# Two transformer blocks on one core: stage boundaries cut into units of two k-tiles, last steps by token block, context normed ahead of its stage

## The reference

```python
# first block
h = rmsnorm(x, pre_mix_g);  p = h @ w_in                        # 4368 columns
o = concat(rmsnorm(window_attention(p)), rmsnorm(forgetting_attention(p)))
x = x + rmsnorm(o @ w_out, post_mix_g)
h = rmsnorm(x, pre_ffn_g);  u = conv3(h @ w_up)                 # 2 * 5632 columns
x = x + rmsnorm((gelu(gate(u)) * val(u)) @ w_down, post_ffn_g)
# second block: six modulation vectors of 2048 from c, and from c_ctx
sh_a, sc_a, g_a, sh_m, sc_m, g_m = split(silu(c) @ w_ada + b_ada)
h  = rms_norm(x, norm_attn_w) * (1 + sc_a) + sh_a
hc = rms_norm(ctx, norm_attn_w) * (1 + csc_a) + csh_a           # 256 context rows
q, k, v, u = split(h @ w_in_2)                                  # 2560 columns; k, v of hc too
x = x + g_a * (concat(attention(q, k, v, kc, vc), pool(u) @ pool_w * pool_scale) @ w_out_2)
x = x + g_m * (relu(modulate(rms_norm(x, norm_mlp_w)) @ w_mlp_up) ** 2 @ w_mlp_down)
return rms_norm(x, final_norm_w)
```

## Time and profile before

| what | value |
|---|---|
| median of 3 runs | 2277.32 us (2276.34 to 2283.1) |
| the profiled execution | 2285.57 us, of it the span 2283.9 us |
| mean granted TensorE clock | 0.974 |
| TensorE busy | 2182.5 us, 96% of the span |
| VectorE, ScalarE, GpSimd busy | 1521.3, 1064.6, 135.2 us |
| mean DMA | 211 GB/s |

### The profile page before, as it was taken

How to read it: one execution, slowest core, us unless ns; L and a number is a source line. 1 busy time by engine, 2 the same in 40 slices (tenths; PEclk the granted TensorE clock), 3 DMA queues, 4 the chain that set the end, 5 groups by cost and what they waited for, 6 DMA issues and landing times.

```text
span 2283.9 us, 30297 instructions
## 1 busy us (share of the span) xinstructions
PE 2182.5 (96%) x10232; PEld 1807.2 (79%) x10232; DVE 1521.3 (67%) x1845; ACT 1064.6 (47%) x1379; POOL 135.2 (6%) x233
## 2 busy tenths in 40 slices
PE   7999998999999999999978999889999999999997
PEld 6888776788778888888867778777888888888876
DVE  6987788687895887768665364556655555655655
ACT  5444654555433554345456355345434434444442
POOL 2101000101010101100000000001000000000000
PEclk9998999999998999999999999899999999999999
DMA  8985077788786888977645250465756756766652
GB/s 283 305 292 188 1 233 263 231 267 267 254 281 207 276 273 276 310 247 240 205 147 184 86 184 1 147 203 192 232 185 211 240 193 211 233 199 205 222 182 94
DMA packets 267022, 482.51 MB, mean 211 GB/s; under 512 B 14861, under 2 KB 107349, under 8 KB 265633
## 3 DMA queue, kind: packets, MB, share of 16 engines
q1 hardware_dynamic: 236544, 367.18, 48.1%
q0 software_dynamic: 30192, 113.72, 15.8%
...
HBM read 478.81 MB, written 2.11 MB: 211 GB/s over the span
## 4 chain that ended last, share of the span: by engine, by line
PE 93%; ACT 3%; DVE 2%; issue 1%; DMA 0%; DVEq 0%; ACTq 0%
PE G L1416 28%; PE G L1418 28%; PE G L1417 28%; PE T L1463 1%; PE T L1600 1%; PE T L1709 1%; PE T L1452 1%; PE T L1541 1%; ACT junk L498 1%; PE G L1689 1%; ACT w_hi L548 1%; PE G L1534 1%; PE T L1564 0%; DVE h_lo L941 0%; PE G L1730 0%
## 5 line engine op out<-in xcount | busy, mean ns | idle before, releaser
L868 DVE TENSOR_TENSOR w_lo<-raw,w_hi 128x1024 fp32r<-128x1024 f32 x696 | 844.0, 1223 | 481.3 <-ACT w_hi L548 477.0
L548 ACT ACTIVATE w_hi<-raw 128x1024 fp32r<-128x1024 f32 x696 | 735.4, 1060 | 913.5 <-PE G L1418 911.1
L1416 PE MATMUL G<-w_hi,h_hi 128*128 128x512 f32 (+1 forms) x1920 | 754.6, 393 | 17.1 <-ACT w_hi L548 7.1
L1418 PE MATMUL G<-w_hi,h_lo 128*128 128x512 f32 (+1 forms) x1920 | 749.4, 390 | 0.0
L1417 PE MATMUL G<-w_lo,h_hi 128*128 128x512 f32 (+1 forms) x1920 | 749.3, 390 | 0.0
L1416 PEld LDWEIGHTS G<-w_hi,h_hi 128*128 128x128 f32 x1920 | 363.9, 190 | 95.1 <-issue 11.3
L1418 PEld LDWEIGHTS G<-w_hi,h_lo 128*128 128x128 f32 x1920 | 363.6, 189 | 75.3
L1417 PEld LDWEIGHTS G<-w_lo,h_hi 128*128 128x128 f32 x1920 | 363.8, 189 | 72.9
L1416 PE MATMUL G<-w_hi,a_hi 128*128 128x512 f32 x896 | 353.4, 394 | 5.6 <-ACT w_hi L548 4.2
L1418 PE MATMUL G<-w_hi,a_lo 128*128 128x512 f32 x896 | 350.8, 392 | 0.0
L1417 PE MATMUL G<-w_lo,a_hi 128*128 128x512 f32 x896 | 350.7, 391 | 0.0
(11 more groups left out here) (233 smaller groups left out, 1173.2 us busy)
## 6 DMA issues: line engine op xcount, KB each, us to landing
ada_w<-in_w_ada POOLq DMA_DIRECT2D x192, 512.0 KB, 5.0
raw<-in_w_up SPq DMA_DIRECT2D x176, 512.0 KB, 6.0
raw<-in_w_mlp_up SPq DMA_DIRECT2D x128, 512.0 KB, 4.7
raw<-in_w_mlp_down SPq DMA_DIRECT2D x128, 512.0 KB, 4.7
raw<-in_w_in SPq DMA_DIRECT2D x104, 512.0 KB, 5.2
raw<-in_w_down SPq DMA_DIRECT2D x88, 512.0 KB, 5.9
raw<-in_w_out SPq DMA_DIRECT2D x64, 512.0 KB, 4.8
raw<-in_w_in SPq DMA_DIRECT2D x8, 272.0 KB, 4.1
```

What stands on the lines that cost most here:

```text
L548: act.activation(w_hi[:, s % 4], raw[:, s // 2 % 4, STEPK * (s % 2):STEPK * (s % 2) + STEPK, :], ACT.Copy).then_inc(hi_ready, 1)
L868: dve.tensor_tensor(w_lo[:, s % 4], raw[:, s // 2 % 4, STEPK * (s % 2):STEPK * (s % 2) + STEPK, :], w_hi[:, s % 4].bitcast(F32), ALU.subtr ...
L1416: pe.matmul(out, ah, wh, start=f, stop=False)
L1418: mm = pe.matmul(out, al, wh, start=False, stop=l)
```

## The change

Units of two k-tiles take the place of groups of four at each boundary (`UNITS = 8`, each unit its own T bank). Where there is no shift, h_hi and h_lo are made straight from PSUM. `begin`, one on each of the three engines, writes transposes, the first three steps, and the weight parts of the next steps between the units. Raw weights lie in 8 slots of 2 k-tiles, and a load is four DMAs of 256 KB.

```diff
@@ load (SyncE)
-            if l >= 4:
-                sp.wait_ge(lo_ready, 2 * l - 6 + 2 * d)
-            for k in range(2):
...
+            for half in range(2):
+                s = 2 * l + half
+                if s >= 8:
+                    sp.wait_ge(lo_ready, s - 7 + 2 * d)
+                for k in range(2):
...
+                        dst, part = raw[:, s % 8, k, 0:src.shape[2]], src[:, STEPK * half + k, :]
+                    sp.dma_start(dst, part).then_inc(raw_full[s % 8], 16)
@@ TensorE
+        def begin(name, src, s, parity, ready):
+
+            turns(name, src, 0, 3)
+            steps(s, 0, 1, parity, H, ready)
+            turns(name, src, 3, 5)
+            steps(s, 1, 2, parity, H, ready)
+            turns(name, src, 5, 7)
+            steps(s, 2, 3, parity, H, ready)
+            turns(name, src, 7, 8)
```

```diff
+        def last_steps(s, acts, kt, ready):
...
+            for b in range(NB):
+                for k in range(2):
+                    for j in range(STEPK):
...
+                        pe.matmul(G[:, 2 + b, :], ah, wh, start=False, stop=False)
...
+                if b == 0:
+                    mm.then_inc(block_done, 1)
```

```diff
-            for k in range(8):
+            for k in range(3 if c == 0 else 0, 7 if c == 3 else 8):
                 lo(s0 + 8 * c + 3 + k)
-                if k % 2:
-                    ada_op(1, 4 * c + k // 2)
+                if (k in (5, 7) if c == 0 else k in (0, 1, 2, 3) if c == 3 else k % 2):
+                    ada_op(2, tile)
+                    tile += 1
```

```diff
+            def context():
+                if c >= 1:
+                    act.wait_ge(ctx_in, 16)
+                    for g in (2 * c - 2, 2 * c - 1):
+                        squares(g, lambda b: cx[:, b, g * N:g * N + N], sums=sqc)
+                if c == 2:
+                    root("ctx")
...
+            pool.tensor_scalar(cx[:, b, :], cx[:, b, :], rstdc[:, b:b + 1], None, ALU.mult).then_inc(ctx_scaled, 1)
...
+            residual(q, (lambda b: u_buf[:, b, (q - 6) * UCOLS:(q - 5) * UCOLS]) if q >= 6 else None)
+            dve.wait_ge(x_new, X_NEW["in2"] + q + 1)
+            in2_scale(q)
...
+        for q in range(UNITS):
+            turn("ctx", cx, q)
+            step(s0 + 8 + q, 1, H, STEPK * q, q == 0, q == 7, None)
```

```diff
+        for q, more in enumerate(((4,), (5, 6), (7,))):
+            steps(s0, q, q + 1, 0, H, r)
+            for m in more:
+                mix(m)
...
+        root("final", rstdx[:])
+        for b in range(NB):
+            for c in (0, 2):
+                dve.tensor_scalar(y[:, b, c * N:c * N + N], y[:, b, c * N:c * N + N], rstdx[:, b:b + 1], None,
```

980 lines of the change are left out of this document (611 added, 369 removed).

## The result

The changed kernel takes 2258.93 us, the median of four runs (2256.68 to 2260.77), beside 2279.47 for the kernel before, measured on the same chip (four runs, 2276.34 to 2283.1). The ratio is 0.9909, with a 95% interval of 0.9889 to 0.9929: it gained 20.5 us, some 16 to 25, where 39.2 were forecast. The time lies 2 us above the range's upper end of 2257.

A forecast was written before the change was run, and what follows sets the result against it. TensorE, busy for 96% of the span, was taken to bound the kernel. Gains less losses by boundary summed to 39.2 us, from the profiled 2285.6 to 2246, or 2238 on the median's scale; range 2224 to 2257.

The forecast's parts named there:

- the context: In the chunk with the context's transposes, transposes need only their units' banks: 8 us saved.
- out2: Attention 2 to out2: attention's half is split first and the mix fills time between steps, 11.5 us saved.
- the end: After the last stage: less work on the path and stores by block leave 11.2 us of 15.0, 3.8 saved.
- the term of -2 from down1c to in2: Boundary before in2: first step at t + 16 (t = previous step's end), but later steps wait; 2 us lost.
- rival C: At the boundaries, units gain less, through GpSimd contention or boundaries 3 us worse each; up to 2257 us, chance 0.18.
- the moved sum, "+1": First modulation sum moved from ahead of attention 1 to behind its scores: 1 us gained, between 0 and 4.
- out1's last two steps, "some 2.6 us": In out1's last chunk, four modulation tiles on VectorE make the last low part come some 2.6 us late.
- out2 to mlp2: Boundary before mlp2: block 0 evacuated early, table loaded ahead, first step at t + 7.2; 5.6 us saved.
- Attention to out1: Attention 1 to out1: first step at t + 4.1, 3.5 of waits, some 2 for the clock; 3.3 us saved.
- B: Before in2: the context does not hold down1c, so in2 begins 7 to 9 us sooner; 2230 us, chance 0.15.
- D: Weight loads: 256 KB DMAs take longer per byte, so TensorE waits; 2256 to 2305 us, chance 0.06.
- E: Last step pairs: VectorE is late, blocks save nothing; 5 us or less gained overall, 2273 us, chance 0.06.

The follow-up runs named there:

- after: The changed kernel itself, against the kernel before: 2258.93 us, ratio 0.9909.
- ctx_half: Changed kernel with GpSimd scaling only block 0 of the context, VectorE block 1 behind in2's units; 2252.11 us, ratio 0.9885 to the kernel before.
- ctx_late: Changed kernel with GpSimd's two context scalings moved behind in2's last unit; 2254.63 us, ratio 0.9896 to the kernel before.
- sum_back: Changed kernel with the first modulation sum put back ahead of attention 1; 2254.74 us, ratio 0.9894 to the kernel before.
- tiles_apart: Changed kernel with out1's last four modulation tiles behind low parts 0, 1, 5, 6, not 0 to 3; 2255.0 us, ratio 0.9871 to the kernel before.
- three: Changed kernel with VectorE scaling the context behind in2's opening, plus the changes of sum_back and tiles_apart; 2238.49 us, ratio 0.9822 to the kernel before.
- plain_last: Changed kernel with the last two steps of out1, down1c, out2, mlp2 not by block; 2259.3 us, ratio 0.9921 to the kernel before.
- loads_512: Changed kernel with raw weights loaded in DMAs of 512 KB, not 256 KB; 2256.7 us, ratio 0.9891 to the kernel before.

## Why the prediction was wrong

**The boundaries** were right, but for the one before in2 and the wait in out1: first steps at t + 4.2, 5.4 and 7.5 for 4.1, 5.7 and 7.2, the context +8.1 for 8, out2 +11.7 for 11.5, the end 10.8 for 11.2 us. Only the first step of in2 was not at t + 16 but at 24.4.

**The step that failed most: contention, in the term of -2 from down1c to in2.** Under rival C the prediction bounded it by nothing and by GpSimd's time of 4 to 8 us in full, and said "I keep the low end in the sum". It is 8.5 us to the first step and 9.9 to in2's third chunk, so even above the upper bound. No row stood behind the 4 to 8: GpSimd took 10.87 for its two scalings. The reason given was that "GpSimd waits only for the context's root and can be through before the second block's products". It waited for that root, but so does the high part that stands behind the root in ScalarE's program: GpSimd started at t + 0.2 and VectorE's low part at t + 0.8. The order of ScalarE's instructions, shown ahead of the prediction, put these two side by side, and the low end of "nothing" was not open. The rule cited there, the Trainium skill, GPSIMD Engine Reference, Specifications, said it: the trace agrees, with a low part of two inputs at 4.16 us for 1.23. The Trainium skill, SBUF — State Buffer, SBUF: two separate sides, is sharper: it has an exclusive lock that whichever comes first keeps for the whole instruction. The traces agree in the main: what was held began its work only 1.9 us before the end of a scaling of 5.44 (after, ctx_half), and in ctx_late GpSimd was the one held. Who came first cannot be read from GpSimd's rough spans.

One more thing in this term was read wrongly and did no harm. The high part behind the context's root was taken for that of down1c's last step. Both parts of that step were there in time, and no wait stands ahead of the last two steps, against what the last part of the prediction wanted to see; the high part is that of in2's second step. Block 0 was still taken only at t + 2.8 without GpSimd, as forecast (t + 3), since the same instruction stands ahead of its evacuation on VectorE: there a right number came out of a wrong reading.

**The second: the moved sum, "+1", between 0 and 4.** No gain, 6.8 us lost, on the wrong side of both ends. Two things were missed. The matmuls cost TensorE their time wherever they stand, 10.7 us inside and 12.0 ahead, against 6.2 by which attention began sooner. And the clock fell behind them: sum_back, which has the sum ahead, has 1.00 where after has 0.56. The clock is the larger part, by what one execution shows. In ctx_half the sum stands inside attention too, but the lower clock held only for some 4 us behind it: its halves took 3.73 and 3.84 us, and from in1's end to attention's end it is 76.2 us, 1.1 more than before and not 6.8. The prediction counted the lower clock only behind idle gaps. The trace of before could have told otherwise. The 10.83 us of the earlier trace rows are themselves a mean of both levels (the two halves at the upper one take 7.6 us), and amid up1b's products a sum of 64 such matmuls begins at 715.16 and takes 11.57 us; around its end and behind it TensorE was busy throughout, at 0.72:

```profile
720.00:740.00 20.00, 20.00 (x82) 17.50 (x83) 12.61 (x21) 3.83 (x5) 0.00 (x0) 0.72 0.34 107
```

**The third: out1's last two steps, "some 2.6 us".** 4.5 and 1.7 of clock. VectorE's sum of four tiles and low parts was right, but it took every tile's load as landed, though VectorE's idle time ahead of such tiles, 62.9 us for one kind of them, stands in the earlier trace rows; the tile at 377.66 was 1.3 us late. In the eight profiled kernels with this order of tiles the steps start 3.3 to 5.0 us late, in tiles_apart and three not at all: the order of the tiles, not their number, makes the wait.

**Smaller ones.** Blocks of the last steps were part of several terms and are worth 2 us in all (plain_last), so the units must be worth more than counted: out2 to mlp2 gave 7.0 for 5.6, of which the blocks are 0.6. Attention to out1 gave 2.3 more than forecast: from attention's end to out1's eighth step it is 29.1 us, of which eight steps at full clock are 21.7 and the first step's 4.2 and 3.2 of waits are the rest, so that most of the 2 us put down for the clock are not there.

**From the trace to the medians.** 39.2 - 7.3 - 8.3 + 1.2 = 24.8, and 4.3 more because the forecast was moved as a whole from an execution that lay 6 to 8 us above its median. It is not shown where that execution lost them. For the changed kernel the spread has one visible source: from in1's end to attention 1's end it takes 76.2 to 86.9 us in the profiled executions of the seven kernels that have the sum where the change put it, and 76.0 to 76.9 in three that have it ahead, one execution each; the lower clock does not hold equally long in each. Of attention's loss 6.8 is therefore one draw.

**The rivals.** C was right in its kind and in its 8 us for the contention (8.5 measured); its other half, boundaries 3 us worse each, was not. B could not be, as in2's first step was held by GpSimd; with that gone it is at t + 15.8, not before 12. D is refuted by loads_512. The rule cited there, the Trainium skill, DMA: Bandwidth & Descriptors, Measured, is for DMAs issued from GpSimd, while SyncE issues these; the 18 us that were estimated from it are not lost here, where raw weights of eight steps lie in slots and TensorE is busy 624.7 of mlp2's 626.0 us. E holds for the blocks at out1 and down1c (0.1 and 0 us); at out2 and the end they were worth 2.0.
